# RWKV-7 / Mamba-2 / PEER decoder step on one core: the closing norms and state-space samples with centring by a product, sums on four column tiles and rstd on a quarter of the columns

## What is computed

```python
    # RWKV-7 branch: norm per head of 64 channels
    mean = jnp.mean(y, axis=-1, keepdims=True)
    var = jnp.mean(jnp.square(y - mean), axis=-1, keepdims=True)
    yn = ((y - mean) * lax.rsqrt(var + RW_LN_EPS)).reshape(B, T, RW_DIM)
    yn = yn * ln_w.astype(f32) + ln_b.astype(f32)
    ...
    out = ((yn + bonus) * g).astype(p.dtype)
    # Mamba-2 branch: gate by silu(z), then norm per group of 512 channels
    y = y.reshape(B, T, SSM_DIM) * jax.nn.silu(z.astype(f32))
    yg = y.reshape(B, T, SSM_GROUPS, SSM_DIM // SSM_GROUPS)
    yg = yg * lax.rsqrt(jnp.mean(yg * yg, axis=-1, keepdims=True) + NORM_EPS)
    out = (yg.reshape(B, T, SSM_DIM) * norm_w.astype(f32)).astype(p.dtype)
```

## Time and profile before

| | |
|---|---|
| median of 3 runs | 4437.52 us (4434.76 to 4447.11) |
| the profiled execution | 4441.11 us, span 4439.5 us |
| PE busy in the span | 4170.6 us (94%) |
| DVE busy | 3179.5 us (72%) |
| ACT busy | 1432.4 us (32%) |
| POOL busy | 1366.4 us (31%) |
| mean granted TensorE clock | 0.969 of full speed |
| DMA | 928 MB, mean 209 GB/s |

### The profile page before, as it was taken

One profiled execution on the slowest core, in us unless ns is written; L12 is line 12 of the kernel. 1 busy time (PEld: TensorE's weight loads), 2 busy tenths in 40 slices (PEclk: granted clock), 3 DMA queues, 4 the chain that ended last, 5 costly groups with the idle time before them and its releaser, 6 DMA issues. The chain is left out here.

```text
span 4439.5 us, 85485 instructions
## 1 busy us (share of the span) xinstructions
PE 4170.6 (94%) x32575; PEld 3789.2 (85%) x32575; DVE 3179.5 (72%) x6008; ACT 1432.4 (32%) x2183; POOL 1366.4 (31%) x1063
## 2 busy tenths in 40 slices
PE   7999999998768989999999998999999999999997
PEld 4888888887537869878888888999999999999996
DVE  5631343444844248899976665999999999999997
ACT  2221222221654222233346674222222222222223
POOL 6433331000032200054433233433434434434430
PEclk9999999999869999999999999999999999999998
DMA  4665666465533311144435546999999999999994
GB/s 170 201 199 189 205 223 213 180 225 165 155 128 112 123 63 34 51 142 143 142 116 179 208 176 239 318 301 301 301 300 300 304 300 298 303 298 300 303 298 157
DMA packets 523005, 928.00 MB, mean 209 GB/s; under 512 B 284033, under 2 KB 351233, under 8 KB 518689
## 3 DMA queue, kind: packets, MB, share of 16 engines
q1 hardware_dynamic: 387024, 549.29, 38.2%
q0 software_dynamic: 80960, 346.96, 23.3%
q10 hardware_dynamic: 54816, 28.85, 2.2%
HBM read 785.79 MB, written 206.30 MB: 223 GB/s over the span
## 5 line engine op out<-in xcount | busy, mean ns | idle before, releaser
L3298 POOL DMA_INDIRECT ex_rows<-expert_rows,ex_here x512 | 586.7, 1146 | 954.7 <-DVE acc_tok L3433 863.9
L3433 DVE SCALAR_TENSOR_TENSOR acc_tok<-ex_rows,ex_wsp,acc_tok 128x1024 f32<-128x1024 f32 x512 | 634.5, 1281 | 0.2 <-issue 0.2
L2665 PE MATMUL ex_psa<-x_dense_high,eg_u_high 128*128 128x288 f32 x2048 | 605.7, 296 | 11.6 <-ACT ex_w L3361 8.5
L2665 PE MATMUL ex_psa<-x_dense_low,eg_u_high 128*128 128x288 f32 x2048 | 605.7, 296 | 0.0
L2665 PE MATMUL ex_psa<-x_dense_high,eg_u_low 128*128 128x288 f32 x2048 | 605.3, 296 | 0.0
L2756 POOL TENSOR_TENSOR eg_u_low<-eg_u,eg_u_high 128x1024 fp32r<-128x1024 f32 x130 | 335.3, 2580 | 798.3 <-ACT eg_u_high L2751 798.3
L3330 PE MATMUL ex_pso<-ex_w_high,ex_v_high 128*128 128x288 f32 x2048 | 441.4, 297 | 8.9 <-DVE acc L3415 8.9
L3361 ACT ACTIVATE ex_w<-ex_psa 128x288 f32<-128x288 f32 x256 | 105.4, 412 | 1056.1 <-PE ex_psa L2665 1056.1
L3330 PE MATMUL ex_pso<-ex_w_high,ex_v_low 128*128 128x288 f32 x2048 | 440.1, 297 | 0.0
L3330 PE MATMUL ex_pso<-ex_w_low,ex_v_high 128*128 128x288 f32 x2048 | 438.9, 296 | 0.0
L3415 DVE TENSOR_TENSOR acc<-ex_pso,acc 128x576 f32<-128x576 f32 x512 | 374.7, 753 | 47.7 <-PE ex_pso L3330 47.7
(11 more groups left out here) (510 smaller groups left out, 9199.4 us busy)
## 6 DMA issues: line engine op xcount, KB each, us to landing
eg_u<-in_u SPq DMA_DIRECT2D x256, 512.0 KB, 3.6
expert_rows<-in_v SPq DMA_DIRECT2D x128, 512.0 KB, 7.0
ex_v<-in_v SPq DMA_DIRECT2D x128, 512.0 KB
weights<-wt_stage SPq DMA_DIRECT2D x9, 4096.0 KB, 13.0
ex_g<-weights SPq DMA_DIRECT2D x128, 288.0 KB
expert_rows<-eg_act SPq DMA_DIRECT2D x256, 128.0 KB, 1.7
proj<-in_out POOLq DMA_DIRECT2D x50, 548.5 KB, 6.4
in_w<-in_w_in SPq DMA_DIRECT2D x50, 512.0 KB, 4.7
```

The lines of the kernel that those rows point to most:

```text
L2665: yield nc.tensor.matmul(out[:, 0:b - a], w[:, kc, :], half[:, kc, a:b], start=n == 0, stop=n == len(passes) - 1)
L3298: pool.indirect_dma_start(rows[i][:, :], None, table, index(here[par][:, t, j:j + 1]), element_offset=ROW_RUNS[t][0]).then_inc(s_row[i], 16)
L3433: v.scalar_tensor_tensor(out=acc_tok[:, t, :], in0=rows[i][:, at:at + D], scalar=wsp[:, i:i + 1], in1=acc_tok[:, t, :], op0=ALU.mult, op1= ...
```

## The change

All of it is in this phase; the rest of the program is the same.

- *Centring by a product.* A matrix `center` = identity minus 1/64 in two blocks of 64 is built by POOL; PE's product of it with `y` is the centred tile, in PSUM (L1942). ACT squares it into `ysq` (L2050) and copies it back to `y` (L2051). DVE's `center` is gone.
- *Sums on four column tiles.* A sum of squares (`quarter_sums`, L1947) is four matmuls of 272 columns. Each has 32 columns of ones as weights and writes its own 32 of the 128 output partitions, so that the four quarters of the columns lie below each other in 128 x 272.
- *rstd on a quarter.* ACT copies these sums to SBUF (`keep_sums`, L2057) and takes Ln and Exp on 272 columns each (L2061, L2065), of several norms in one instruction where they are ready together: pairs 0 and 1; group 0; pairs 2, 3 and group 1.
- *Spread.* PE brings the rstd back to 128 x 1088 by five matmuls with a selection matrix `pick` (L1968), into one PSUM buffer that DVE reads in the norm (L2146) and the scaling (L2161). The next spread waits until it has been read.
- *Silu.* ACT takes `Silu` of `z` in place (L2044). POOL's product and the sigmoid buffer are gone.
- *Samples.* The differences of the log decays are two wide instructions (L2178, L2180) instead of 16; products over two groups are one instruction; the skip term is one product ahead (L2188) and one add (L2197) instead of eight fused ones. The heads write to bank 0 of `ss_ps`, so the first state product waits for the skip add.
- *Transfers.* Both `y` tiles are loaded first, then the state, then gates and bonuses, with semaphores of their own.
- *Order.* The lists of PE, ACT and DVE are woven anew; group 0 is scaled before the norms of pairs 2 and 3.

```diff
@@ def phase_ssd_samples_and_post(k, smp, oa, ob, d, z, mw):
+    QT = T // COL_TILES
+    CENTER_AT, SPREAD_AT = 448, 240
+    CENTER_CHUNKS = ((0, 512 - CENTER_AT), (512 - CENTER_AT, 1024 - CENTER_AT), (1024 - CENTER_AT, T))
+    SPREAD_CHUNKS = ((0, 0, QT), (1, QT, 2 * QT), (2, 2 * QT, 1024 - SPREAD_AT), (2, 1024 - SPREAD_AT, 3 * QT), (3, 3 * QT, T))
+    SLOT = {"rw0": 0, "rw1": 1, "so0": 2, "rw2": 0, "rw3": 1, "so1": 2}
+    EARLIER = {"rw2": "rw0", "rw3": "rw1", "so1": "so0"}
+    RSTD_OF = {"rw0": "rw01", "rw1": "rw01", "so0": "so0", "rw2": "last", "rw3": "last", "so1": "last"}
...
-                for i in range(KC):
-                    pool.wait_ge(SA.sem, SA.done("sigmoid", i))
-                    nc.gpsimd.tensor_tensor(z[:, i, :], z[:, i, :], sg[:, :], ALU.mult).then_inc(*SU.inc("silu"))
...
+                def centered(p_, kept=None):
+                    pe.wait_ge(s_y[p_ % 2], 16 * (p_ // 2 + 1))
+                    if kept:
+                        at(KEPT, kept)
+                    else:
+                        pe.wait_ge(s_ctr, 4)
+                    for a, b in CENTER_CHUNKS:
+                        mm = nc.tensor.matmul(center_ps[:, a:b], center[:, :], y[p_ % 2][:, a:b], start=True, stop=True)
+                    mm.then_inc(s_cen, 1)
+
+                def quarter_sums(ones, src, start, stop):
+                    for q in range(COL_TILES):
+                        mm = nc.tensor.matmul(sum_ps[col_tile(q), :], ones, src[:, q * QT:q * QT + QT], start=start, stop=stop)
                     return mm
...
+                def head_sums(p_):
+                    pe.wait_ge(s_cp, p_ + 1)
+                    quarter_sums(pair_sum, ysq, True, True).then_inc(*SUM.inc(f"rw{p_}"))
+
+                def group_sums(g, kept):
+                    at(KEPT, kept)
+                    for i in range(GT * g, GT * g + GT):
+                        pe.wait_ge(s_sq, i + 1)
+                        mm = quarter_sums(k.ones[:, 0:COL_TILE], sq[i % 3], i % GT == 0, i % GT == GT - 1)
+                        if i % GT < GT - 1:
+                            mm.then_inc(s_used, 1)
+                    mm.then_inc(*SUM.inc(f"so{g}"))
+
+                def spread(of, read):
+                    at(RS, RSTD_OF[of])
+                    if read:
+                        pe.wait_ge(*read)
+                    for q, a, b in SPREAD_CHUNKS:
+                        mm = nc.tensor.matmul(spread_ps[:, a:b], pick[:, q, :], rs[:, SLOT[of], a - q * QT:b - q * QT], start=True, stop=True)
+                    mm.then_inc(*SPR.inc(of))
...
-                mean(0)
+                centered(0)
+                head_sums(0)
+                centered(1, "rw0")
                 pe.wait_ge(s_S, 16)
                 at(DV, "w")
                 heads(0, 4)
-                var(0)
-                heads(4, 8)
-                mean(1)
-                heads(8, 12)
-                var(1)
+                head_sums(1)
+                heads(4, 12)
+                pe.wait_ge(s_pick, 3)
+                spread("rw0", None)
                 heads(12, 16).then_inc(*PE.inc("y"))
-                mean(2)
+                spread("rw1", (s_norm, 1))
                 at(AC, "btok")
                 at(DV, "xd")
+                at(DV, "skip")
                 states(0)
-                total(0)
                 states(1)
-                total(1)
-                var(2)
+                group_sums(0, "rw1")
                 states(2)
-                total(2)
+                centered(2, "so0")
                 states(3)
-                mean(3)
-                total(3)
+                spread("so0", (s_norm, 2))
+                head_sums(2)
                 states(4)
-                total(4)
+                centered(3, "rw2")
                 states(5)
-                var(3)
-                total(5)
+                head_sums(3)
                 states(6)
-                total(6)
                 states(7)
-                total(7)
+                group_sums(1, "rw3")
+                spread("rw2", (s_n, GT))
+                spread("rw3", (s_norm, 3))
+                spread("so1", (s_norm, 4))
...
+                def silu(i):
                     act.wait_ge(k.s_z[i // 4], 128)
-                    if i:
-                        act.wait_ge(SU.sem, SU.done("silu", i - 1))
-                    a.activation(sg[:, :], z[:, i, :], ACT.Sigmoid).then_inc(*SA.inc("sigmoid"))
+                    a.activation(z[:, i, :], z[:, i, :], ACT.Silu).then_inc(s_silu, 1)
 
                 def centered_square(p_):
-                    act.wait_ge(RD_.sem, RD_.done("center", p_))
+                    act.wait_ge(s_cen, p_ + 1)
                     if p_:
-                        act.wait_ge(RD_.sem, RD_.done("norm", p_ - 1))
-                    a.activation(rw_rs[:, :], y[p_ % 2][:, :], ACT.Square).then_inc(*RA.inc("sq"))
...
+                        at(SUM, f"rw{p_ - 1}")
+                    a.activation(ysq[:, :], center_ps, ACT.Square).then_inc(s_ysq, 1)
+                    a.activation(y[p_ % 2][:, :], center_ps, ACT.Copy).then_inc(s_cp, 1)
+
+                def keep_sums(of):
+                    at(SUM, of)
+                    if of in EARLIER:
+                        at(SPR, EARLIER[of])
+                    a.activation(rs[:, SLOT[of], :], sum_ps, ACT.Copy).then_inc(*KEPT.inc(of))
```

More of the change, by code:

```diff
@@ L1844, in phase_ssd_samples_and_post @@
         s_gp = k.sem("so_prompt_gated")
-        s_r = k.sem("so_rstd_step")
         s_n = k.sem("so_scaled")
+        s_pick = k.sem("po_pick_step")
+        s_ctr = k.sem("po_center_step")
+        s_silu = k.sem("so_silu_done")
+        s_sq = k.sem("so_square_done")
+        s_cp = k.sem("ro_centered_kept")
+        s_ysq = k.sem("ro_square_done")
+        s_cen = k.sem("ro_centered")
+        s_used = k.sem("so_square_summed")
+        s_norm = k.sem("ro_normed")
+        s_bonus = k.sem("ro_bonus_added")
+        s_gate = k.sem("ro_gated")
         PE = Progress(k.sem("ss_pe"), "col", "bc", "x", "y")
         AC = Progress(k.sem("ss_act"), "excs", "col", "btok", "dec")
-        DV = Progress(k.sem("ss_dve"), "cb", "x", "diff", "end", "ce", "xd", "w", "skip")
-        RP = Progress(k.sem("ro_pe"), "mean", "var")
-        RA = Progress(k.sem("ro_act"), "sq", "ln", "rstd")
-        RD_ = Progress(k.sem("ro_dve"), "center", "norm", "bonus", "gate")
-        SP = Progress(k.sem("so_pe"), "sum")
-        SA = Progress(k.sem("so_act"), "sigmoid")
-        SQ = Progress(k.sem("so_square"), "sq")
-        SU = Progress(k.sem("so_silu"), "silu")
+        DV = Progress(k.sem("ss_dve"), "cb", "x", "diff", "min", "end", "ce", "xd", "w", "dx", "skip")
+        SUM = Progress(k.sem("po_sum"), "rw0", "rw1", "so0", "rw2", "rw3", "so1")
+        KEPT = Progress(k.sem("po_sum_kept"), "rw0", "rw1", "so0", "rw2", "rw3", "so1")
+        LN = Progress(k.sem("po_ln"), "rw01", "so0", "rw23", "so1")
+        RS = Progress(k.sem("po_rstd"), "rw01", "so0", "last")
+        SPR = Progress(k.sem("po_spread"), "rw0", "rw1", "so0", "rw2", "rw3", "so1")
         at_of = lambda eng: (lambda S_, step: eng.wait_ge(S_.sem, S_.done(step)))
@@ L1889, in _ @@
                 at = at_of(pe)
-                def product(out, ones, src, start, stop):
-                    for a, b in TOK_CHUNKS_BANKED:
-                        mm = nc.tensor.matmul(out[:, a:b], ones, src[:, a:b], start=start, stop=stop)
-                    return mm
-                def mean(p_):
-                    pe.wait_ge(k.s_rw_in[p_ % 2], 48 * (p_ // 2 + 1))
-                    if p_:
-                        pe.wait_ge(RA.sem, RA.done("ln", p_ - 1))
-                    product(ps_rw, k.pairones[:, :], y[p_ % 2], True, True).then_inc(*RP.inc("mean"))
@@ L2086, in gated @@
-                    dve.wait_ge(RD_.sem, RD_.done("bonus", p_))
-                    v.tensor_tensor(oa[:, p_, :], yt, gate[h][:, :], ALU.mult).then_inc(*RD_.inc("gate"))
+                                           op1=ALU.add).then_inc(s_bonus, 1)
+                    dve.wait_ge(s_bonus, p_ + 1)
+                    v.tensor_tensor(oa[:, p_, :], yt, gate[h][:, :], ALU.mult).then_inc(s_gate, 1)
                 def gate_prompt(i):
-                    dve.wait_ge(SU.sem, SU.done("silu", i))
+                    dve.wait_ge(s_silu, i + 1)
@@ L2140, in _ @@
                 at(PE, "y")
[L2141 to L2144 removed]
+                at(DV, "dx")
+                v.tensor_tensor(ob[:, :, SEQ:T], ob[:, :, SEQ:T], yv, ALU.add).then_inc(*DV.inc("skip"))
                 at(DV, "skip")
                 v.tensor_tensor(ob[:, :, SEQ:T], ob[:, :, SEQ:T], z[:, :, SEQ:T], ALU.mult).then_inc(s_skip, 1)
[L2147 removed]
```

213 lines of the change are left out of this document (110 added, 103 removed).

## The result

The changed kernel takes 4419.82 us (median of 6 runs, 4409.82 to 4422.66); the kernel before took 4440.12 us beside it (6 runs, 4434.76 to 4447.11). The ratio is 0.9948, 95% interval 0.9936 to 0.996: faster, by 20 us of 4440, half a per cent and clear of the scatter. Forecast were 4416.5 us, 4403 to 4431, and 21 us less. The profiled execution of the changed kernel has a span of 4416.3 us against 4439.5, and the phase alone makes it: from its first instruction to the first of the merge it takes 110.25 us instead of 133.56. (What lies ahead of the phase was 4.0 us longer in this execution and what lies behind it 3.9 shorter; the program is the same there.)

What follows compares the result with a forecast made beforehand. The phase was taken to be bound by a chain of short waits between engines; the new chain ends at 1333.5 instead of 1354.5, 21 us less, which off the median of 4437.5 gives 4416.5 us, range 4403 to 4431.

Steps and rivals of the forecast that it cites:

- Start to the samples' output: Phase start to the samples' output: centrings 4.0 us each, heads 4.44 a quarter, a quarter sum 1.05; output at 1262.1.
- To the gated columns: Samples' output to gated columns: 11.7 us of DVE steps from the first spread, plus 7 us from meeting POOL's decays; 1276.3.
- price of the silu step: ACT's silu in one instruction, priced at a sigmoid's 1.11 us; 21.1 us of POOL's products, for which DVE waited, gone.
- To the first scaling: Gated columns to first scaling: ACT's squares and rstd, PE's state products and sums; spread ends at 1292, before 1330.
- nearly at the high level: PE's clock from gated columns to first scaling: state products, sums and centring 12.2 us at high level, 23.3 at low.
- Quarter sums: PE's sums of squares: four products on column tiles run side by side, 0.55 us or 1.05 a group.
- D: Rival on PE's sums: column tiles go one after the other, clock as forecast; 14 us back, 4430.5 us; chance 0.08.
- E: Rival on PE's sums: tiles one after the other, each switch draining, low clock; 29 us slower, 4466 us; chance 0.04.
- Tail: Last rstd at 1313 to scalings' end at 1333.5: all spreads wait for that rstd, first and last 4.25 us each.
- Rival B: POOL's decays miss DVE and PE stays at the high clock level: 15 us more gained, 4402 us; chance 0.16.
- C: Rival: PE at the low clock level throughout, costing 15 us; 6 us less than before, 4431 us; chance 0.12.
- The table loads: ACT's loads fall from 17 to 9, five on the chain; next activation 1.30 us after each starts, no drain added.

Runs made afterwards that it cites:

- experiment 3: The kernel before with silu alone changed: ACT takes Silu in place, POOL's product is gone; 4443.57 us, ratio 1.0006.
- experiment 5: The kernel before with Silu on ACT and POOL's decays held back until the sample columns are gated; 4440.63 us, ratio 0.9995.
- experiment 2: The changed kernel with silu as before: sigmoid on ACT, product on POOL, taking turns; 4424.89 us, ratio 0.9958.
- experiment 1: The changed kernel with all four quarters of a sum on one column tile, one after the other; 4424.18 us, ratio 0.9969.
- experiment 7: The changed kernel with five unread products of 512 columns added on PE ahead of the three end spreads; 4421.39 us, ratio 0.9949.
- experiment 6: The changed kernel with the rstd of pairs 2 and 3 in an exponential of its own; 4414.96 us, ratio 0.9941.
- experiment 9: The changed kernel with decays held back, the pairs' own exponential, and the last group's sums ahead of the last states on PE; 4397.95 us, ratio 0.9899.
- experiment 4: The changed kernel with POOL's decays held back until the sample columns are gated on DVE; 4414.12 us, ratio 0.9935.

## Why the prediction was right

Each point is counted from the phase's start, forecast against profile. Samples' output: 40.9 and 38.6. Sample columns gated: 55.1 and 50.4. First scaling: 70.8 and 67.7. Last rstd: 91.8 and 90.1. End of the last scaling: 112.3 and 110.0. The sum was 21 us and the phase gave 23.3, the medians 20.3.

*Start to the samples' output*, 2.3 us too much. The first centring took 2.21 us and not 4.0, but nothing came of that: ACT had an exponential of the samples in front of its square, and the heads waited for the state's transfer until 17.9 us, 0.1 later than forecast. What came sooner were the heads: the first quarter took 2.6 us instead of 4.44 and the sum behind it 0.67 instead of 1.05, at a granted clock of 1.00, which had still been 0.50 in the second centring just ahead and was 0.51 again in the quarters that followed.

*To the gated columns*, 2.4 us too much. The mechanism was right and its size wrong: the decays cost DVE 4.3 us, not 7. Experiments 3 and 5 show the mechanism at full size, 11.5 us on seven steps. My price of the silu step was also right (1.11), but not my picture of what it replaced: by experiment 2 taking turns with POOL would have held the samples' output back by 9.4 us, through ACT's order.

*To the first scaling*, 1.6 us too little: PE wasn't "nearly at the high level". The first eight state products took 7.16 us, at the low one, behind 6.53 us of idling. From there to the last rstd, 22.4 instead of 21.0.

*Quarter sums.* "Four side by side" was right: 0.67 us at the high level, between the two values 0.55 and 1.05 that I took for the two clocks. With it rivals D and E fall; experiment 1 is D built, and it cost 10.3 us where I had put 14 (13.2 where the sums are exposed, less 2.9 that came back elsewhere).

*Tail.* 19.9 us instead of 20.5 to the scalings' end: the first spread mostly and the last wholly at the low level (3.68 and 4.28 for my 4.25). The middle one (2.24) lies beside DVE's bonus and gate, as forecast. That the price is the clock's is shown by experiment 7.

*Rival B* fell on both conditions, *C* on the windows' clock of 0.63 to 0.76 (the earlier trace rows had 0.52 to 0.77). *The table loads*, nine now, behave as before: the load at 1227.96 took 1.28 us and the silu stands at 1229.26, 0.02 us behind its end. The drain that the Trainium skill ("ScalarE: Activation LUTs", What ACT_TABLE_LOAD costs) adds doesn't show. Of the drain that the Trainium skill has for a change of tiling mode ("TensorEngine Tiling (Array Packing)", Key Properties) the trace shows none either: at 1246.29 a head product begins 0.60 us after the sum at 1245.69, which took 0.67.

The errors were 4.7 us too much up to the gating, 3.0 too little up to the last rstd and 0.6 too much in the tail, and so partly cancel: that the sum is off by only 2.3 us is in part luck. What I didn't see at all is how much the change left: the single exponential for pairs and group, which saves two table loads (2.6 us), put all three spreads and both norms behind the last sums. With an exponential of its own for the pairs, the phase is 2.0 us shorter in experiment 6; with the sums in the right place as well, experiment 9 gains 8.8 us behind the gated columns. How much of the 12.8 us from experiment 9 is the held-back decays' was measured only in the changed order (1.1, experiment 4), not in the new one, where they are part of the 4.0 us up to the gated columns.

## What to carry to other kernels

In a phase bound by waits, a removed operation on one engine frees the next one on it to start earlier: look up what that will meet, before counting the gain (silu alone made the phase 6 us longer). Batching small steps to save a table load is only worth it while nothing large waits for the last member of the batch. When a wait is moved ahead, look at which buffer release now stands behind it in the same queue: between experiments 6 and 9 PE's order and the decays' start changed, and the phase went from 108 to 97 us.

## What was not expected of the hardware

DVE steps with both inputs in SBUF, next to POOL's decays from SBUF, took 2.87 to 2.98 us instead of 1.2 to 1.35, nearly the length of a decay more. In the same stretch norms that read PSUM kept their 1.34 to 1.35 us (at 1267.63 in the changed kernel), and the add that reads PSUM its 0.68. Where a DVE step had begun first, it kept its time and the decay paid: the bonus at 1269.01 took 1.35, and the decay that began beside it at 1269.13 took 2.98 us instead of 1.90. The Trainium skill ("SBUF — State Buffer", SBUF: two separate sides) describes an exclusive lock of a shared pair of ports, held for a whole instruction and taken by DVE only with two SBUF inputs or in a fast mode; these rows agree. The sixteen short subtractions in the samples' part of the kernel before took 7.29 us beside POOL's silu products and 2.68 in experiment 3, without them; which of the two cases of that page they are, if either, is not shown. Products of 512 columns whose result nobody reads, in PE's idle time, brought the spread behind them from 3.7 to 4.3 us down to 2.24 to 2.27.
